# First layer's first modulation section: loaded in two halves by columns, with the first projection's weights between them

## The reference

```
m = silu(cond) @ w_mod[l] + b_mod[l]              # 1024 -> 6144: shift1, scale1, gate1, shift2, scale2, gate2
h = rmsnorm(x, g_mix[l]) * (1 + scale1) + shift1
h @ w_in[l]                                       # aq, ak, av, mq, mk, mv, mo and the gates of the mLSTM
x = x + gate1 * mixer(...) @ w_out[l]
h = rmsnorm(x, g_ffn[l]) * (1 + scale2) + shift2
x = x + gate2 * moe(h)                            # 16 experts, 2 of them for each token
```

## Time and profile before

| What | Value |
|---|---|
| Median of 3 runs | 879.25 us (878.8 to 882.39) |
| Profiled execution | 879.01 us, span 877.1 us |
| TensorE matmuls busy | 828.5 us, 94% of the span |
| VectorE, ScalarE, GpSimd busy | 267.8, 180.3, 46.8 us |
| Read from HBM | 286.44 MB, 329 GB/s over the span |

### The profile page before, as it was taken

How to read it: one execution, slowest core, us unless ns; L and a number is a source line. 1 busy time by engine, 2 the same in 40 slices (tenths; PEclk the granted TensorE clock), 3 DMA queues, 4 the chain that set the end, 5 groups by cost and what they waited for, 6 DMA issues and landing times.

```text
span 877.1 us, 10786 instructions
## 1 busy us (share of the span) xinstructions
PE 828.5 (94%) x4394; PEld 465.5 (53%) x4396; DVE 267.8 (31%) x503; ACT 180.3 (21%) x356; POOL 46.8 (5%) x51
## 2 busy tenths in 40 slices
PE   4899999898999999999989999979799999999998
PEld 3374657675444554455444645868554554355444
DVE  0220468225321122212222306842631122202223
ACT  3321225215101110111032203630611110111011
POOL 0500311001000000000000005000010000000000
PEclk9999999999999999999999999989799999999999
DMA  8995579559799999999999634405749999999992
GB/s 355 374 367 223 192 308 396 186 183 423 299 399 424 427 430 427 427 428 430 423 408 354 249 139 162 185 25 192 274 178 400 424 429 424 429 430 427 428 430 83
DMA packets 41076, 289.32 MB, mean 330 GB/s; under 512 B 3337, under 2 KB 5697, under 8 KB 23633
## 3 DMA queue, kind: packets, MB, share of 16 engines
q1 hardware_dynamic: 39312, 285.30, 79.8%
q0 software_dynamic: 1488, 3.44, 1.3%
q10 hardware_dynamic: 240, 0.08, 0.0%
HBM read 286.44 MB, written 2.37 MB: 329 GB/s over the span
## 4 chain that ended last, share of the span: by engine, by line
PE 87%; DMA 5%; DVE 3%; ACT 3%; issue 1%; SPq 0%; DVEq 0%; ACTq 0%
PE ps L991 25%; PE ps L661 14%; PE ps L1019 13%; PE ps L979 7%; PE ps L914 7%; PE ps L1030 6%; DMA ring<-in_w_in 5%; PE ps L673 3%; PE ps L580 3%; ACT xe L1360 1%; PE ps L790 1%; ACT hT L1180 1%; PE ps L815 1%; PE ps L617 0%; PE ps L847 0%
## 5 line engine op out<-in xcount | busy, mean ns | idle before, releaser
L991 PE MATMUL ps<-ring,xe 128*64 128x512 f32 x1024 | 222.6, 592 | 0.0
L991 PEld LDWEIGHTS ps<-ring,xe 128*64 128x64 f32 x1024 | 73.8, 137 | 145.0 <-issue 144.7
L661 PE MATMUL ps<-ring,hT 128*128 128x512 f32 (+1 forms) x320 | 125.3, 551 | 4.4 <-DMA ring<-in_w_in 4.4
L1019 PE MATMUL ps<-ring,hidT 128*64 128x512 f32 x512 | 113.4, 595 | 0.0
L661 PEld LDWEIGHTS ps<-ring,hT 128*128 128x128 f32 x320 | 60.4, 190 | 66.7 <-issue 58.4
L1799 DVE COPY ye<-ps 128x512 f32<-128x512 f32 x16 | 11.1, 692 | 213.3 <-PE ps L1019 213.3
L979 PE MATMUL ps<-pick,htok 128*128 (+1 forms) x512 | 66.6, 286 | 7.4 <-ACT xe L1360 3.5
L1019 PEld LDWEIGHTS ps<-ring,hidT 128*64 128x64 f32 x512 | 35.3, 137 | 66.9 <-issue 65.5
L979 PEld LDWEIGHTS ps<-pick,htok 128*128 128x128 f32 x512 | 63.4, 200 | 11.9 <-ACT xe L1360 6.8
L1030 PE MATMUL ps<-scat,ye 128*128 (+1 forms) x256 | 59.9, 386 | 0.0
L914 PE MATMUL ps<-hT,ring 128*128 128x256 f32 x256 | 59.2, 391 | 0.0
(11 more groups left out here) (258 smaller groups left out, 636.6 us busy)
## 6 DMA issues: line engine op xcount, KB each, us to landing
ring<-in_w_e_gate SPq DMA_DIRECT2D x32, 2048.0 KB, 12.9
ring<-in_w_e_up SPq DMA_DIRECT2D x32, 2048.0 KB, 16.4
ring<-in_w_e_down SPq DMA_DIRECT2D x32, 2048.0 KB, 11.9
ring<-in_w_mod SPq DMA_DIRECT2D x24, 2048.0 KB, 11.6
ring<-in_w_in SPq DMA_DIRECT2D x10, 2048.0 KB, 21.1
ring<-in_w_out SPq DMA_DIRECT2D x4, 2048.0 KB, 10.4
ring<-in_w_in SPq DMA_DIRECT2D x2, 1024.0 KB, 20.9
C<-in_state_C POOLq DMA_DIRECT2D x2, 512.0 KB, 7.1
```

The lines of the kernel that those rows point to most:

```text
L661: mm = pe.matmul(bank[:, 0:width], hT[:, k, b * P:(b + 1) * P], w[:, k, :], start=(k == 0), stop=(k == KD - 1))
L991: mm = pe.matmul(ps[1 + u][64 * j:64 * j + 64, :], xe[:, k, j * SLOTS:(j + 1) * SLOTS], w[j][:, k, :], start=(k == 0), stop=(k == KD - 1))
L1019: mm = pe.matmul(ps[3 - half][64 * j:64 * j + 64, :], hidT[:, k, j * SLOTS:(j + 1) * SLOTS], w[j][:, k, half * 512:(half + 1) * 512], star ...
```

## The change

Section (0, 0) is split by columns in two: (0, 0) keeps chunks 0 to 3 and 8 to 11, and a new section (0, 0.5) has chunks 4 to 7 and 12 to 15. Each has two slots, with four k rows by two ranges of 512 columns; a slot is loaded by two DMAs of 1 MB, one for each range, in pieces of 2 KB. The load order becomes: (0, 0) slot 0, constants, x, (0, 0) slot 1, `mk`, (0, 0.5) slots 0 and 1, `mq`, `mv` and so on. TensorE does (0, 0), its columns, the products of `mk` with chunks 0 to 3 for both inputs, then (0, 0.5) and its columns, and then the products of `mk` with chunks 4 to 7. ScalarE and VectorE modulate four chunks of both inputs at a time, and VectorE scales both inputs before the columns of the first half. The columns of every section are now added by two instructions, each for half of the chunks.

```diff
+SECTION_CHUNKS = {(l, s): (16 * s, 8, 16 * s + 8) for l in range(DEPTH) for s in range(3)}
+SECTION_CHUNKS[0, 0], SECTION_CHUNKS[0, 0.5] = (0, 4, 8), (4, 4, 12)
+SECTION_CHUNKS[1, 2], SECTION_CHUNKS[1, 3] = (32, 4, 36), (40, 4, 44)
...
         for g in PROJ:
             put((g, l))
+            if l == 0 and g == "mk":
+                for i in range(section_slots(0, 0.5)):
+                    put(("mod", 0, 0.5, i))
...
+                    own = slice(k * i, k * (i + 1))
+                    if second == first + chunks:
+                        load(("mod", l, s, i), w_mod[l, :, own, first * P:(first + 2 * chunks) * P], k=k)
+                    else:
+                        load(("mod", l, s, i), w_mod[l, :, own, second * P:(second + chunks) * P], k=k,
+                             other=w_mod[l, :, own, first * P:(first + chunks) * P])
...
+                if other is not None:
+                    sp.dma_start(dst[:, :, 0:WB], other).then_inc(range_landed[int(4 * key[2]) + key[3]], 16)
+                    dst = dst[:, :, WB:2 * WB]
                 sp.dma_start(dst, src).then_inc(slot_landed[slot], 16)
...
-            load_section(0, 0, 1, 2, 3)
+            load_section(0, 0, 1)
...
                     load((g, l), w_in[l, :, :, c0:c0 + width], width)
+                    if l == 0 and g == "mk":
+                        load_section(0, 0.5)
...
+                def first_half_then_rest():
+
+                    w = landed(("mk", 0)).rearrange("p (k n) -> p k n", k=KD)
+                    for half in range(2):
+                        for b in range(NB):
+                            bank = begin((("mk", b), 0)) if half == 0 else ps[banks[("mk", b), 0][0]]
+                            for k in range(4 * half, 4 * half + 4):
+                                ready = h_v if k % 2 else h_a
+                                pe.wait_ge(ready, 4 * half + 2 * b + k // 2 - 2 * half + 1)
+                                mm = pe.matmul(bank[:, :], hT[:, k, b * P:(b + 1) * P], w[:, k, :],
+                                               start=(k == 0), stop=(k == KD - 1))
+                            if half == 1:
+                                done((("mk", b), 0), mm)
+                        if half == 0:
+                            section_rows(0, 0.5, 0, 1)
+                            section_columns(0, 0.5)
...
-                project("mk", (0,), fresh=True)
-                for sec in early_sections(l):
-                    section_rows(*sec, 3)
-                project("mk", (1,), fresh=True)
-                for sec in early_sections(l):
-                    section_columns(*sec)
+                if l == 0:
+                    first_half_then_rest()
+                else:
+                    project("mk", (0,), fresh=True)
...
                 if l == 0:
-                    section_row(0, 0)
-                act.wait_ge(mod_ready, 2 * l + 1)
...
+                    for half in range(2):
+                        section_row(0, (0, 0.5)[half])
+                        act.wait_ge(mod_ready, half + 1)
+                        act.wait_ge(xr_ready, 3)
+                        for b in range(NB):
+                            modulate(l, 0, sq, b, (4 * half, 4 * half + 2))
...
+                for half, at in enumerate((first, second)):
+                    span = slice(at, at + chunks)
+                    ins = dve.tensor_tensor(modc[:, l % 2, span, :].rearrange("p (g j) b -> p g j b", g=2),
+                                            bank[:, 0:n * P].rearrange("p (j g r) -> p g j r", j=n, g=4)[:, 2 * half:2 * half + 2, :, 0:NB],
+                                            per_col(cols[:, l, span].rearrange("p (g j) -> p g j", g=2), NB), ALU.add)
+                ins.then_inc(free(key), 1)
...
                 if l == 0:
-                    modulation_columns(0, 0)
...
+                    scaled(sq, 1, 0, KD)
+                    for half in range(2):
+                        modulation_columns(0, (0, 0.5)[half])
+                        dve.wait_ge(mod_ready, half + 1)
+                        dve.wait_ge(xr_ready, 3)
+                        for b in range(NB):
+                            modulate(l, sq, b, (4 * half + 1, 4 * half + 3))
```

More of the change, by code:

```diff
@@ L93, in shape_constants, with amplitudes @@
     return out
-SECTION_CHUNKS = {(l, s): (16 * s, 16) for l in range(DEPTH) for s in range(3)}
-SECTION_CHUNKS[1, 2], SECTION_CHUNKS[1, 3] = (32, 8), (40, 8)
+SECTION_CHUNKS = {(l, s): (16 * s, 8, 16 * s + 8) for l in range(DEPTH) for s in range(3)}
+SECTION_CHUNKS[0, 0], SECTION_CHUNKS[0, 0.5] = (0, 4, 8), (4, 4, 12)
+SECTION_CHUNKS[1, 2], SECTION_CHUNKS[1, 3] = (32, 4, 36), (40, 4, 44)
 def section_slots(l, s):
-    return SECTION_CHUNKS[l, s][1] // 4
+    return SECTION_CHUNKS[l, s][1] // 2
 def section_reads(l, s, i):
     return sum(section_slots(*sec) - 1 for sec in SECTION_CHUNKS if sec < (l, s)) + i
+def amplitudes(l, which):
+    return 2 + 2 * l + which
 def early_sections(l):
@@ L141, in bank_plan @@
         put(("x", r), r)
-    put(("modrow", 0, 0), 7)
-    put(("modcol", 0, 0), 7)
+    for half in (0, 0.5):
+        put(("modrow", 0, half), 7)
+        put(("modcol", 0, half), 7)
     for l in range(DEPTH):
@@ L367, in build @@
         gate_in = sem("gate_in")
+        range_landed = [sem(f"range_landed{i}") for i in range(4)]
         layer_in, state_out = sem("layer_in"), sem("state_out")
@@ L483, in load_section @@
             def load_section(l, s, *which):
-                first, chunks = SECTION_CHUNKS[l, s]
+                first, chunks, second = SECTION_CHUNKS[l, s]
                 n = section_slots(l, s)
@@ L488, in load_section, with load @@
                 for i in which or range(n):
-                    load(("mod", l, s, i), w_mod[l, :, k * i:k * (i + 1), first * P:(first + chunks) * P], k=k)
-            def load(key, src, width=WB, k=KD):
+                    own = slice(k * i, k * (i + 1))
[4 more added lines that the diff above has]
+                             other=w_mod[l, :, own, first * P:(first + chunks) * P])
+            def load(key, src, width=WB, k=KD, other=None):
                 slot, _, last = weights[key]
@@ L1189, in _ @@
                 if l == 0:
-                    section_row(0, 0)
-                act.wait_ge(mod_ready, 2 * l + 1)
[L1192 to L1196, removed]
+                    for half in range(2):
[4 more added lines that the diff above has]
+                            modulate(l, 0, sq, b, (4 * half, 4 * half + 2))
+                else:
+                    act.wait_ge(mod_ready, amplitudes(l, 0))
+                    for b in range(NB):
+                        act.wait_ge(xr_ready, XR_STEPS * l + 1 + 2 * b)
+                        modulate(l, 0, sq, b, (0,))
+                        act.wait_ge(xr_ready, XR_STEPS * l + 2 + b)
+                        modulate(l, 0, sq, b, (2, 4, 6))
                 for b in range(NB):
@@ L1329, in _ @@
                 rms(l, 1)
-                act.wait_ge(mod_ready, 2 * l + 2)
+                act.wait_ge(mod_ready, amplitudes(l, 1))
                 act.wait_ge(xr_ready, XR_STEPS * l + 4)
@@ L1421, in modulation_columns @@
                 bank = full(dve, key)
[L1422 to L1427, removed]
-                taken(dve, key)
[L1429 to L1432, removed]
+                first, chunks, second = SECTION_CHUNKS[l, s]
+                n = section_slots(l, s)
+                for half, at in enumerate((first, second)):
[4 more added lines that the diff above has]
+                ins.then_inc(free(key), 1)
+                taken(dve, key)
+                if s in (0, 0.5, 2):
+                    which, scale, g = (1, 4 * KD, A_GFFN) if s == 2 else (0, KD, A_GMIX)
+                    lo, hi = (0, KD) if (l, s) not in ((0, 0), (0, 0.5)) else (first, first + chunks)
+                    dve.scalar_tensor_tensor(amp[:, l % 2, which, lo:hi, :], modc[:, l % 2, scale + lo:scale + hi, :], 1.0,
+                                             per_col(cols[:, l, g + lo:g + hi], NB), ALU.add, ALU.mult).then_inc(mod_ready, 1)
             def scaled(square, b, lo, hi):
@@ L1452, in normalise @@
                 if l == 0:
-                    modulation_columns(0, 0)
[L1454 to L1459, removed]
+                    scaled(sq, 1, 0, KD)
[3 more added lines that the diff above has]
+                        dve.wait_ge(xr_ready, 3)
+                        for b in range(NB):
+                            modulate(l, sq, b, (4 * half + 1, 4 * half + 3))
+                else:
+                    dve.wait_ge(mod_ready, amplitudes(l, 0))
+                    dve.wait_ge(xr_ready, n + 2)
+                    modulate(l, sq, 0, (1, 3, 5, 7))
+                    scaled(sq, 1, 0, KD)
+                    dve.wait_ge(xr_ready, n + 3)
+                    modulate(l, sq, 1, (1, 3, 5, 7))
             def residual(l, name, gate, which=range(4)):
```

11 lines of the change are left out of this document (9 added, 2 removed).

## The result

The changed kernel took 890.08 us (median of 6 runs, 888.2 to 896.27), the kernel before beside it 881.36 (878.8 to 884.62). The ratio is 1.0099, with a 95% interval of 1.0069 to 1.0128: 8.7 us slower, where 7.6 were forecast, and the median lies 0.6 above the range. The forecast stood on the profiled execution of before, 879.0; before's median beside the changed kernel was 2.4 more. The profiled execution took 889.34 us, its span is 887.5, against 877.1 before. So the traces have 10.4 us to explain.

A forecast was written before the change was run, and what follows sets the result against it. TensorE's work was taken as 87% of the chain of waits, so the end moves with `mk`'s end: 6.1 us later plus 1.5 for low clock, +7.6 on 879.0, gives 886.6 us, range 880.5 to 889.5.

The forecast's parts named there:

- The direction and its cause in the start: At the start: GpSimd's small loads move with `mk` onto the second half's slots, delaying the last to 41.8; kernel slower, chance 0.75.
- The second hand-over: Between the last slot's rows and `mk`'s second half: an additional copy, transposes, columns and first chunk, 2.1 us.
- The sum for the start: Up to the end of `mk`: 6.1 us later, plus 1.5 for TensorE's low clock, +7.6 us.
- x at 12.64: Start: x, queued behind the first slot in 2 KB pieces, lands 0.41 us later than the 12.23 of before.
- To 35.45: Start: the first half of `mk`'s products runs from 28.45 for 7.0 us, ending at 35.45.
- the thin stretch ahead of 28.45: Before `mk`'s first products, in the slot-in-time rival: low clock there gives 882.3 instead of 880.6; case chance 0.20.
- The wait for the second slot: 4.5 us: After the second half's first slot, TensorE waits from 37.3 to 41.8 for its last slot: 4.5 us.
- the 1.5 of clock: Behind the wait for the last slot, its 1.82 us of rows may run at half speed: 0 to 1.8, taken as 1.5.
- from there the same distances as before: From the gates on: the start's delay is passed on with the same distances as before, nothing added.
- all other sections keep their loads: Sections after the start: loads unchanged, one more addition of 0.19 each for columns, nothing or at most 0.8 us in all.
- The rival of a longer loss: At the start: low clock after both pauses and a second slot later than `mv` was, total beyond 889.5; chance 0.04.

The follow-up runs named there:

- e1: The changed kernel, but GpSimd's small loads wait for the last slot of the second half instead of for `mk`; ratio 1.0069 to before.
- e3: The kernel before with each slot of section (0, 0) loaded by four DMAs of 512 columns (2 KB pieces), order kept; ratio 1.0028 to before.
- e4: The changed kernel with four idle TensorE matmuls in the pause before `mk`'s first products; ratio 1.0111 to before.
- e2: The kernel before with seven idle matmuls put ahead of `mk`'s products, to make TensorE later from there on; ratio 1.0106 to before.
- e6: The changed kernel with 124 waits without work ahead of the constants' landing, 256 TensorE instructions more than before in all; ratio 1.0065 to before.
- e9: The kernel before with 132 waits without work spread over product steps of `mv`, `aq` and `mo`; ratio 1.0031 to before.
- e10: The kernel before with 198 waits without work spread over product steps of `mv`, `aq` and `mo`; ratio 1.0009 to before.
- e8: The kernel before with 172 waits without work put ahead of the constants' landing; ratio 1.0088 to before.
- e7: The changed kernel with 40 waits without work ahead of the constants' landing, 172 TensorE instructions more than before in all; ratio 1.0107 to before.
- e11: The changed kernel with small loads behind the second half, four idle matmuls before the first products and 48 spread waits, 198 instructions over before; ratio 1.0039 to before.
- e5: The kernel before with 132 waits without work put ahead of the constants' landing; ratio 1.0040 to before.

## Why the prediction was wrong

**The direction and its cause in the start held.** The second half's slots do stand where `mq` and `mv` stood, GpSimd's loads do move onto them, and e1 shows that they hold the last one up. It landed at 40.9 (forecast 41.8). The second hand-over took from 42.9 to 44.96, 2.06 us (2.1), and the second half of `mk` 7.13 (7.0). The sum for the start was 6.1 and 1.5 for the clock, 7.6; the traces have 5.5.

**Terms that were mis-sized there.**
- x at 12.64: it was 13.24. Its issue came 0.9 us later than before (4.04 against 3.18), but in e3 it came at 4.99 and x landed at 12.64, so the cause isn't shown. With the first slot's rows at 3.06 the first products started at 29.36, not 28.45.
- "To 35.45": the first products took 8.8, not 7.0. I named the thin stretch ahead of 28.45 as a cause of low clock in a rival only. It decides here, as it makes TensorE arrive at 40.0, nearly with the slot.
- "The wait for the second slot: 4.5 us" and the 1.5 of clock behind it: 0.94 and none. A kernel that keeps its clock has the wait, as e4 shows (4.25), and behind it loses more clock than I allowed (3.3, where my bound was 1.8, since the low clock reached into the products). The losses stand in for one another: what the low clock takes, the wait gives back.

**The step that failed** is the one that passes the start's loss on and adds nothing: "from there the same distances as before", with "all other sections keep their loads" and the additional instructions at nothing. 5.5 us were passed on one to one up to the experts, and 4.9 more were added behind: 0.4 in the experts of layer 0, 2.8 in the transition, 1.8 in the rest. e2 has a part of it (1.3 in the transition) without any piece of the change, e6 takes it out of the change's transition, and e9 and e10 switch the pause on and off in the kernel before.

What I had put at nothing is the length of TensorE's program ahead of that point. Rows ran ahead of the pause, 12 or 9 of them, with 0, 256 and 7 instructions more than before. None did with 28, 132, 150, and 172 in e8. There was no pause with 198, and with 172 in e7.

What lies there is a jump: behind the experts' last pair TensorE skips the code for overfull experts, which is not run. The Trainium skill ("Runtime: NRT & Kernel Launch", Instruction fetch mechanics) says that instructions are fetched in blocks of 256 by a DMA queue of the engine's own, ahead only in sequence, and that a jump out of the blocks at hand stalls. The traces agree. 256 instructions more restore before's rows to the instruction, with one transfer more on q8 (27 against 26; it is 26 with 7 and 28 more, 27 from 132 on). The distance counts in single instructions: 12 rows ahead, and 9 with 7 instructions more. And in all ten traces with a pause there is one q8 transfer of 1.1 us that begins 0.6 to 1.4 us after TensorE's last work ahead of the jump, and TensorE goes on 1.4 to 1.6 us after its end. From that last work to going on it is 3.3 to 4.1 us in all ten; where rows of the target had come with an earlier transfer, they fill the first 1.5 to 1.9 of it. In the three traces without a pause the last transfer ahead of the rows began earlier: 2.7 us ahead of them in e7, 6.1 in e10, 6.0 in e11. The profile names no releaser for the pause; that the transfer ends it is read from these times.

The pause, with rows that run partly at the low clock behind it (4.9 to 5.3 us instead of 3.6), costs 1.3 to 1.4 us of the transition in e2, e4, e5 and e8. With the clock low over all 32 rows it costs up to 3.2 (28.3 against 25.1 in e1). It isn't all lost, since before waits 2.30 us for the landing of `mk` where these kernels don't.

**The number.** The median missed the range by 0.6, and 2.4 of the 3.5 us between 886.6 and 890.08 are the kernel before itself, which took 881.36 beside the change and not 879.0. That the difference of 8.7 us came near the 7.6 of the forecast is luck: in the traces the start gave 2.1 less than I had added up and the rest 4.9 more. The rival of a longer loss had two reasons, low clock after both pauses and a slot later than `mv` was. At the start the clock fell after the first pause alone, and the slot came earlier.

**What stays open.** At 172 the two kernels differ (e7 no pause, e8 one): e7's transfer began at 453.75, before TensorE had done its last work ahead of the jump (456.44), e8's at 455.15, after it (454.17). Why, no run shows, so the number of instructions alone does not settle it. The pause in layer 1's last pair (1.1 to 1.6 us) appears in all seven traces with 132 to 172 additional instructions and in none of the six with 0 to 28, 198 or 256, where it is at most 0.23. So it goes with the program's length too, though its row names the landing of `w_e_up`; the way there isn't shown. Nor is the rest of what lies behind layer 1's gates, where against before the changed kernel has 1.8 us more, e9 4.5 and e10 none. And the traces of the kernel before and its kin differ in the clock at `mk`'s start (14.00, 15.42, 15.62 us), so some 1.5 us of the 10.4 may be chance of the one trace of before; the interval of the ratio, 6.1 to 11.3 us, has room for it.

## What to carry to other kernels

When work is moved ahead of a landing, look at what else is triggered by that landing: here GpSimd's loads were tied to `mk` and came along onto the one transfer that TensorE was waiting for. An overlap gains only what the engine that sets the end is idle. In e11, its cleanest form, the second hand-over took 2.1 us and the gates came 1.2 later, so the overlap itself gained 0.9. Before a difference of under 1% is put down to a change's mechanism, compare the distances between fixed points over the whole trace, look at the instruction queue around each pause that ends with "issue", and pad the program by instructions that do nothing, since a jump further on may see only the program's length.

## What the runs showed of the hardware

- Instructions without work moved the total by some 3 us either way: 132 in the kernel before cost 0.31% (e9, interval 0.07 to 0.55), 124 in the changed one gave back 0.34% (e6 against the change, two ratios whose intervals overlap).
- After the jump TensorE could go on 1.4 to 1.6 us after a 16 KB transfer of the instruction queue had ended, 3.3 to 4.1 us after its last work ahead of the jump (ten traces).
- TensorE's clock and waits are coupled: in e4's trace the clock was kept up in one pause, the next wait grew to 4.25 us, and behind it the clock was low and 3.3 us were lost instead of 1.7.
- Pieces of 2 KB in place of 8 KB cost 0.44 us for each 2 MB (e3), and x came 0.6 to 1.0 us later in the change, e1, e4, e7 and e11, which have one DMA more ahead of it; with three more (e3) it came only 0.4 later.
- An instruction that only waits on semaphores long reached is not free ahead of a start: 172 of them put the first slot's rows from 15.84 to 23.89 (e8). TensorE's first matmul came at 15.41 with 132 of them, at 14.56 with 124 and at 19.73 with 172, so I estimate 0.11 us for each, counted from 0.7.
